# Splitting weights ahead of the norms, first activation parts ahead of weight splits, and context loads behind weight loads

## The reference

```
x   = x   + 0.5 * m[2]  * swiglu(modulate(rmsnorm(x,   norm_ffn1), m[0],  m[1]),  w_ffn1_in, w_ffn1_out)
ctx = ctx + 0.5 * mc[2] * swiglu(modulate(rmsnorm(ctx, norm_ffn1), mc[0], mc[1]), w_ffn1_in, w_ffn1_out)
px, pc = modulate(rmsnorm(x or ctx, norm_mix), ...) @ w_mix_in     # attention and short convolution
x   = x + m[5] * (mix @ w_mix_out)
x   = x + 0.5 * m[8] * swiglu(modulate(rmsnorm(x, norm_ffn2), m[6], m[7]), w_ffn2_in, w_ffn2_out)
x   = rmsnorm(x, final_norm)
# second block, with its own context ctx_2
feats = modulate(rmsnorm(x or ctx_2, norm1_w), ...) @ w_in          # retention and gated linear attention
x   = x + g1 * (y @ w_out)
x   = x + g2 * peer_ffn(modulate(rmsnorm(x, norm2_w), ...))         # 16 of 16,384 experts x 8 heads per token
out = rmsnorm(x, norm_f_w)
```

## Time and profile before

| What | us |
|---|---|
| median of three runs | 3168.67 |
| profiled execution, whole | 3173.42 |
| its span | 3171.6 |
| TensorE busy | 2752.9 (87%) |
| VectorE busy | 1723.3 (54%) |
| GpSimd busy | 1161.6 (37%) |
| ScalarE busy | 890.4 (28%) |

### The profile page before, as it was taken

The page is one execution under the profiler, slowest core; times in us unless marked ns, Lnnn a source line. Parts: engine busy times, 40 slices in busy tenths (PEclk is TensorE's granted clock), DMA queues, the critical chain, the costliest instruction groups (busy, mean ns, idle before and its releaser), DMA issues.

```text
span 3171.6 us, 30128 instructions
## 1 busy us (share of the span) xinstructions
PE 2752.9 (87%) x11118; PEld 1893.7 (60%) x11118; DVE 1723.3 (54%) x3643; ACT 890.4 (28%) x1683; POOL 1161.6 (37%) x763
## 2 busy tenths in 40 slices
PE   6899999989978999989987889988777777777876
PEld 4899989977657887778846665544333322222332
DVE  3777652032737603231146467766776777677765
ACT  3111123123533223242132333223322222222221
POOL 1222222223924444333210245445444444444442
PEclk8999999989998999989997899999999999999999
DMA  5455531212014523311100279999999999999997
GB/s 204 150 178 177 178 124 55 62 64 70 25 67 139 179 93 93 100 47 60 55 34 1 67 277 393 387 418 416 427 427 427 427 427 427 427 427 427 427 427 298
DMA packets 126957, 722.12 MB, mean 228 GB/s; under 512 B 15204, under 2 KB 17516, under 8 KB 60140
## 3 DMA queue, kind: packets, MB, share of 16 engines
q0 software_dynamic: 73728, 536.90, 40.6%
q1 hardware_dynamic: 37448, 127.67, 11.7%
q10 hardware_dynamic: 15652, 55.90, 5.6%
HBM read 718.31 MB, written 2.10 MB: 227 GB/s over the span
## 4 chain that ended last, share of the span: by engine, by line
PE 58%; DMA 26%; DVE 9%; ACT 3%; issue 3%; POOL 1%; SPq 0%; ACTq 0%; DVEq 0%; POOLq 0%
PE acc L582 14%; PE acc L583 13%; PE acc L584 13%; DMA wring<-in_peer_rows,squares 8%; DMA hid<-in_peer_rows,squares 8%; PE sums L1063 4%; DMA arena<-in_peer_rows,squares 4%; PE acc L1063 3%; DMA resid<-in_peer_rows,squares 3%; PE sums L515 2%; DMA modw<-in_peer_rows,squares 1%; DVE hid L1758 1%; ACT hid L1124 1%; DVE hid L2362 1%; DVE squares L1817 1%
## 5 line engine op out<-in xcount | busy, mean ns | idle before, releaser
L2527 POOL TENSOR_TENSOR wring_parts<-wring,wring_parts 128x1024 fp32r<-128x1024 f32 (+1 forms) x215 | 522.8, 2443 | 1269.6 <-ACT wring_parts L1124 1269.3
L582 PE MATMUL acc<-hid_parts,wring_parts 128*128 128x384 f32 (+2 forms) x2088 | 770.6, 369 | 56.1 <-DVE hid_parts L1764 31.4
L584 PE MATMUL acc<-hid_parts,wring_parts 128*128 128x384 f32 (+2 forms) x2088 | 753.4, 361 | 0.0
L583 PE MATMUL acc<-hid_parts,wring_parts 128*128 128x384 f32 (+1 forms) x1656 | 598.7, 362 | 0.0
L582 PEld LDWEIGHTS acc<-hid_parts,wring_parts 128*128 128x128 f32 (+1 forms) x2088 | 396.7, 190 | 118.4 <-issue 54.0
L584 PEld LDWEIGHTS acc<-hid_parts,wring_parts 128*128 128x128 f32 (+1 forms) x2088 | 396.3, 190 | 36.2
L1124 ACT ACTIVATE wring_parts<-wring 128x1024 fp32r<-128x1024 f32 (+1 forms) x215 | 222.2, 1040 | 567.4 <-DMA wring<-in_w_ffn_out 214.5
L583 PEld LDWEIGHTS acc<-hid_parts,wring_parts 128*128 128x128 f32 x1656 | 314.8, 190 | 33.2 <-issue 5.5
L2539 POOL DMA_INDIRECT arena<-in_peer_rows,squares x180 | 194.5, 1080 | 234.6 <-PE acc L1063 141.0
L1124 ACT ACTIVATE hid<-hid 128x2 f32<-128x2 f32 (+2 forms) x293 | 67.0, 229 | 759.7 <-DVE arena L2362 234.9
L2539 POOL DMA_INDIRECT wring<-in_peer_rows,squares x158 | 179.1, 1134 | 219.1 <-PE acc L1063 163.5
(11 more groups left out here) (408 smaller groups left out, 4440.4 us busy)
## 6 DMA issues: line engine op xcount, KB each, us to landing
wring<-in_w_ffn_in SPq DMA_DIRECT2D x88, 512.0 KB, 4.9
modw<-in_w_ada ACTq DMA_DIRECT2D x56, 512.0 KB, 3.9
modw<-in_w_mod ACTq DMA_DIRECT2D x48, 512.0 KB, 3.9
wring<-in_w_ffn_out SPq DMA_DIRECT2D x32, 512.0 KB, 3.5
wring<-in_w_in SPq DMA_DIRECT2D x28, 512.0 KB, 3.4
wring<-in_w_mix_in SPq DMA_DIRECT2D x18, 512.0 KB, 3.4
wring<-in_peer_w_q SPq DMA_DIRECT2D x16, 512.0 KB, 5.7
hid<-in_w_ada SPq DMA_DIRECT2D x6, 1024.0 KB, 16.8
```

The costliest lines, as they stand in the source:

```text
L582: nc.tensor.matmul(o, wh, high, start=first, stop=False)
L583: nc.tensor.matmul(o, wh, low, start=False, stop=False)
L584: return nc.tensor.matmul(o, wl, high, start=False, stop=last)
L2527: nc.gpsimd.tensor_tensor(Wlor[:, p, 0:blocks, 0:cols], Wlo[:, p, 0:blocks, 0:cols], Whir[:, p, 0:blocks, 0:cols], ALU.subtract).then_inc( ...
```

## The change

There are six edits.

1. **SyncE.** The load of the second context is passed to `ffn_in` as a function and called behind the first four tile loads of ffn2_in.
2. **Where high parts lie.** The two tiles of high parts in modw are now f = 2 and 3 instead of 18 and 19, and the early parts of the first stage are f = 0, 1, 2, 3. The hid tiles serve f = 4 to 19.
3. **Weight splits of ffn_out's chunks 2 and 3.** In both feed-forward stages they no longer follow the last silu; they stand behind the first four of the remaining parts in `ff_parts`.
4. **Weight splits at the norms.** The first two tiles of the next stage are split in `behind_chunks`, ahead of the squares of tiles 6 and 7. The other two: behind the shift of tiles 1 and 4 at the mix norm, and ahead of all squares at the second block's entry.
5. **Modulation quarters 0 and 1** are multiplied ahead of the wait for the first silu, instead of behind the first gating.
6. **The decay numbers** (18 small operations on 8 or 4 columns, VectorE L1892 to L1903) move from ahead of `swiglu` to behind the first stage's `ff_parts`.

```diff
         hi_ff768 = ([(tmp_parts[:, 0:HALF], tmp_parts[:, HALF:TC]), (rstd_parts[:, 0:HALF], rstd_parts[:, HALF:TC])]
+                    + [(modw_parts[:, TC * f:TC * f + HALF], modw_parts[:, TC * f + HALF:TC * (f + 1)]) for f in range(2)]
                     + [(hid_parts[:, TC * f:TC * f + HALF], hid_parts[:, TC * f + HALF:TC * (f + 1)]) for f in range(16)]
-                    + [(modw_parts[:, TC * f:TC * f + HALF], modw_parts[:, TC * f + HALF:TC * (f + 1)]) for f in range(2)]
...
-        EARLY_PARTS = {"ffn1_out": [0, 1, 18, 19], "ffn2_out": [0, 1, 2, 3, 4, 5]}
+        EARLY_PARTS = {"ffn1_out": [0, 1, 2, 3], "ffn2_out": [0, 1, 2, 3, 4, 5]}
...
-                    if j == 2 and weights is not None:
-                        high_part(weights)
+                    if j in weights:
+                        high_part(weights[j])
...
-                    if u % halves == halves - 1:
+                    if u % halves == halves - 1 and u < units * FT // 2 - 1:
                         for m in range(2):
                             high_part(s0 + W_RING + 2 * (u // halves) + m)
...
-                for f in PARTS[name][len(EARLY_PARTS[name]):]:
+                for i, f in enumerate(PARTS[name][len(EARLY_PARTS[name]):]):
+                    if i == 4:
+                        for q in range(2, W_RING):
+                            high_part(TILE_OF[name] + q)
...
-                for q in range(3 * j + W_RING, min(3 * j + W_RING + 3, OUT_TILES)):
+                for q in range(3 * j + W_RING, min(3 * j + W_RING + 3, OUT_TILES + 2)):
                     high_part(TILE_OF[name] + q)
...
-            stat(KD, TC, lambda j: behind_chunks("ffn1_out", j, TC), meanwhile=range(s0, s0 + W_RING), only=1)
-            shift(1, hi768r, lo768, 3 * KD, TC, 2)
+            stat(KD, TC, lambda j: behind_chunks("ffn1_out", j, TC), only=1)
+            shift(1, hi768r, lo768, 3 * KD, TC, 2, {1: s0 + 2, 4: s0 + 3})
...
-            stat(KD, TC, renormed, meanwhile=range(s0, s0 + W_RING))
+            for s in range(s0 + 2, s0 + W_RING):
+                high_part(s)
+            stat(KD, TC, renormed)
...
+                if first_pair == 0:
+                    mod_quarter(0)
+                    mod_quarter(1)
                 for u in range(2 * sides * FT // 2):
...
-                    if pair < stop_pair:
+                    if pair < stop_pair and (u or first_pair):
...
                 step(0)
+                behind_first()
                 with sp.Fori(1, FT // 2) as i:
                     step(i)
...
-            sp.wait_ge(acc_ready, UNIT["ffn2_in"])
-            for r in range(2):
-                sp.dma_start(tok2[:, r, :], a["ctx_2"][0][r * P:(r + 1) * P, :]).then_inc(tok2_loaded, 16)
-            ffn_in("ffn2_in", a["w_ffn2_in"], 1)
+
+            def second_context():
+                sp.wait_ge(acc_ready, UNIT["ffn2_in"])
+                for r in range(2):
+                    sp.dma_start(tok2[:, r, :], a["ctx_2"][0][r * P:(r + 1) * P, :]).then_inc(tok2_loaded, 16)
+            ffn_in("ffn2_in", a["w_ffn2_in"], 1, second_context)
```

More of the change, by code:

```diff
@@ L1173, in inverse, with shift @@
                 run(rstd[:, 0:t], logs[:, 0:t], ACT.Exp, scale=-0.5).then_inc(rstd_ready, 1)
-            def shift(norm, high, low, tile, t, stage, weights=None):
+            def shift(norm, high, low, tile, t, stage, weights={}):
                 act.wait_ge(mods_ready, stage)
@@ L1443, in _ @@
             behind("mix_out", x_, 0)
-            shift(2, hi512r, lo512, 6 * KD, T, 2, TILE_OF["ffn2_in"] + W_RING - 1)
+            shift(2, hi512r, lo512, 6 * KD, T, 2, {2: TILE_OF["ffn2_in"] + W_RING - 1})
             for x in range(2):
@@ L1599, in _ @@
             behind("w_out", x2_, 2)
-            shift(4, hi512r, lo512, ADA_TILES + 3 * KD, T, 3, TILE_OF["peer_q"] + W_RING - 1)
+            shift(4, hi512r, lo512, ADA_TILES + 3 * KD, T, 3, {2: TILE_OF["peer_q"] + W_RING - 1})
             def query(t):
@@ L1888, in _ @@
             scale(0, hi768r, lo768, lo768r, TC, 0)
+            swiglu("ffn1_in", HALF, 2, 0, 0, EARLY_PAIRS, "ffn1_out", ff768, hi_ff768, lo_ff768, 0)
+            ff_parts("ffn1_out", ff768, hi_ff768, lo_ff768, 0)
             dve.wait_ge(decay_exp, 1)
@@ L1903, in _ @@
             link(V.tensor_scalar(dec[:, 20:24], dec[:, 12:16], 640.0 + P, None, ALU.mult))
-            swiglu("ffn1_in", HALF, 2, 0, 0, EARLY_PAIRS, "ffn1_out", ff768, hi_ff768, lo_ff768, 0)
-            ff_parts("ffn1_out", ff768, hi_ff768, lo_ff768, 0)
             modulation(2, FIRST_GROUPS + EARLY_PAIRS, FIRST_MODS, EARLY_TILES, [(1, "norm_mix", 4 * KD), (2, "norm_ffn2", 7 * KD)],
@@ L2614, in stage_load, with ffn_in @@
                     tile_load(TILE_OF[stage] + t, w, t, P if t < w.shape[0] - 1 else last)
-            def ffn_in(name, w, halves):
+            def ffn_in(name, w, halves, behind_first=lambda: None):
                 s0 = TILE_OF[name]
```

## The result

The changed kernel takes 3137.27 us (median of 4 runs, 3128.56 to 3142.12); the kernel before, run beside it, 3170.18 (4 runs, 3161.62 to 3173.68). The ratio is 0.9896, 95% interval 0.9869 to 0.9923, so 1.0% faster. A second set on another occasion gave 3136.89 against 3171.69, ratio 0.9893 (0.9877 to 0.9911). The prediction was 3138.0 from a sum of 30.7 us. The profiled execution took 3140.62, 32.8 less than before's 3173.42, and it is read here.

A forecast was written before the change was run, and what follows sets the result against it. TensorE's holes were taken to bound the first 1,840 us, DMA transfers the rest. Terms 13.3 + 6.4 + 2.8 + 0.3 + 5.1 + 2.8 = 30.7 us, off the median 3168.7, gave 3138.0; range 3127 to 3153.

The forecast's parts named there:

- Edit 1, 13.3 taken: Behind mix_out: tile loads leave before the context load, so TensorE's sum starts sooner; gain 12.1 to 13.9 us, 13.3 taken.
- Edits 2 and 3 in ffn1_out, 6.4 taken: ffn1_out's first unit: more parts ready ahead of the hole, and no clock fall; gain 6.4 us, bounds 5.2 and 7.6.
- The hold-up near the end: ffn1_out: the split of chunk q = 4 blocks VectorE for one operation nearer the end; 0.6 us lost.
- Edit 3 in ffn2_out, 2.8 taken: ffn2_out: four parts now stand ahead of ScalarE's second split; gain 2.8 us, bounds 1.0 and 4.6.
- Edit 4a: Mix norm: first matmul 4.7 us earlier, but the third unit's hole grows to 5; net 0.3, bounds -1.4 and 1.2.
- Edit 4b: Second block's entry: earlier logarithm, scaling freed of two hold-ups; gain 5.1 us taken, bounds 1.0 and 5.5.
- The step that lets the sums start 0.8 later: Second block's entry: splits ahead of the squares meet VectorE's eight multiplications, adding 0.8 us to the start of the sums.
- Edits 5 and 6, 2.8 taken: Modulation quarters: their chain moves earlier and the later decay numbers cost nothing; gain 2.8 us, bounds 1.0 and 4.0.
- Rival (b): Whole kernel: shorter holes keep the clock at its upper level, every upper bound is reached; 3132 us, chance 0.08.
- Rival (a): Gains outside the context-load edit: GpSimd's weight splits block VectorE, shrinking them to about 3 us; 3152 us, chance 0.12.
- rival (c): Behind mix_out: the first tile's load still leaves only behind unit 7, losing 13.3 us; 3162 to 3168 us, chance 0.05.
- rival (d): Output stages and mix_out: ScalarE's waits for loads delay squares, slower from a landing of 46 us; 3180 us, chance 0.03.

The follow-up runs named there:

- edit 3 alone: The kernel before with only the feed-forward weight splits moved behind four parts, early parts still f = 0, 1, 18, 19; 3164.31 us, one run.
- 4b alone: The kernel before with only the second block's entry changed: two weight splits ahead of the norm, two ahead of its squares; 3174.09 us, one run.
- edits 2 and 3 alone: The kernel before with only the modw parts as f = 2 and 3 and the feed-forward weight splits behind four parts; 3161.44 us, one run.
- the two alone: The kernel before with only modulation quarters 0 and 1 ahead of the first silu and decay numbers behind the parts; 3175.08 us, one run.

## Why the prediction was right, step by step

**Edit 1, 13.3 taken, 15.1 measured (15.5 by leaving it out, 17.0 alone).** The mechanism was right: loads landed in 3.4 us, the near end of the landings taken. The size was off in two steps. I added up to a microsecond for the third split on GpSimd in the way of the last addition and for a late load; neither came, the hole is 2.23 and not 3.05 (16.35 - 13.3). And the clock: the sums took 2.07 us before and 1.13 now, another 0.9.

**Edits 2 and 3 in ffn1_out, 6.4 taken, 6.8 measured.** The hole fell by 7.01 - 1.84 = 5.2 and the clock stayed up, 1.6. The hold-up near the end that I took off (0.6) cannot be seen.

**Edit 3 in ffn2_out, 2.8 taken, 4.9 measured.** Four parts ahead of the splits shortened the hole by 2.6, the 2.8 of the step. The fall of the clock, which I had kept for the upper bound, went as well: 2.3. This term is mis-sized, and beyond its bound (4.6) by 0.3. That the fall went was luck: edit 3 alone kept it, behind the same hole.

**Edit 4a, 0.3 taken, 0.3 measured.** The hold-ups came where the step put them, at 2.1 us each (2.87 less 0.74), once on the way to the third unit's accumulators and once more; waits 4.35 and 4.67 where "4 to 5" and "about 5" were forecast. By the rule of the Trainium skill cited in the prediction (SBUF — State Buffer, "Who interferes with whom") the two kinds of instruction exclude each other. The trace agrees: each held operation ends about 0.5 us behind GpSimd's. The cost is the time for which they overlap, 2.1 us, since the operations started 0.1 to 0.4 us into GpSimd's 2.4 to 2.7. The full length would have given a loss of 0.3, and there was none.

**Edit 4b, 5.1 taken, 6.3 measured (5.6 by 4b alone).** The logarithm starts when the sums end (0.05 us behind, before 2.1), and the scaling has no operation over 1 us: the wait fell from 10.26 to 4.34. The step that lets the sums start 0.8 later, since the multiplications meet GpSimd, was right: they took 8.78 for 5.38, and the sums followed the first of them by 3.0 us instead of 1.7. In the profiled run this is hidden, as the multiplications themselves began 1.7 sooner behind the sum of ffn2_out, and the sums came 0.4 sooner, not later. That is the clock and not the edit. From the sum to the first multiplication, before, after, and in the second trace of the changed kernel:

```profile
1340.06:1346.12 6.06, 4.55 (x18) 3.17 (x18) 2.60 (x5) 1.32 (x2) 0.00 (x0) 0.72 0.33 132
```

```profile
1309.85:1314.22 4.37, 2.87 (x18) 2.10 (x18) 2.59 (x5) 3.18 (x4) 0.84 (x1) 1.00 0.44 178
```

```profile
1309.02:1314.94 5.92, 4.42 (x18) 3.04 (x18) 2.59 (x6) 3.21 (x4) 1.44 (x1) 0.73 0.33 134
```

TensorE waited 2.23 us ahead of this place in all three. With edits 2 and 3 alone, without 4b, the upper level lies here too, and the sums come 6.05 us behind ffn2_out's; after, they come 7.36 behind it. In the second trace of the changed kernel they come at 8.31, before at 7.73. So the hold-up costs 0.6 to 1.3 us, and I had taken 0.8. It follows that a part of the 6.3 is the clock's. With the lower level here f fell from 47.1 (before) to 41.4 (the second trace), by 5.7; with the upper one from 44.1 (edits 2 and 3 alone) to 40.8 (after), by 3.3. The 5.1 taken lies between the two.

**Edits 5 and 6, 2.8 taken, 3.4 measured (4.3 by the two alone).** Quarter 2 starts at 87.42, the load landing as worked out; the first sum stands at 115.80, forecast "near 116". The cover of the decay numbers held: b shows no trace of them.

**What the sum missed.** The terms came to 36.8 against the 30.7 taken, near 37, the sum of their upper bounds, though not term by term. Of these 6.1 us, 0.9 behind mix_out and 2.3 in ffn2_out are the clock, and a part of what 4b shows is too. Then 4.3 were given back between the entry and the expert queries, a stretch of which I had said nothing, because no edit touches it. The hit at 3137 to 3138 is in part these two cancelling, which is luck; that each hole fell for its own cause, and by about what was worked out, is not. Rival (b), the clock giving more, names much of what the terms had too little, but its 3132 did not come, since the clock also took back. Rival (a) is refuted by b, e and f, rival (c) by the hole of 2.23 (its bound was off besides: 3168.7 less 9 is 3160, not 3162), rival (d) by the landing of 3.4.

## What to carry to other kernels

An in-order queue is read by what stands behind its longest wait: the context load cost 15 us although nobody wanted it, as it stood ahead of tiles that everybody wanted. If a consumer starts early and then stands still, look whether the pieces that it gets first are those it asks for first; here the renumbering was worth more in ffn1_out (4.3 us) than the reordering (2.7). Judge an edit of a few microseconds by the stretch between two events around it, not by the whole time of one run: two edits here took 4 to 7 us out of their stretch, and their single runs were no faster than the kernel before.

## What was not expected of the hardware

- The same hole, about 2.1 us, was followed by the lower level of the clock in one kernel (0.59 over 4.2 us) and by the full one in another (1.00). Behind 1.90 us it fell (0.52 over 3.4 us), behind 2.07 (1350.68) it did not. Even two executions of one kernel differ: behind the wait of 2.23 us at the end of ffn2_out the granted clock up to the first multiplication was 1.00 in one trace of the changed kernel and 0.73 in the other. The hole of 1.90 us, before:

```profile
698.31 0.70 PE L582 MATMUL acc<-hid_parts,wring_parts 128*128 128x512 f32 x1 [1.90 <-ACT arena L1124]
```

- A stretch that no edit touches took 423.8 us twice in the kernel before, 428.1 and 427.7 in the changed one, and 433.5 in a kernel whose last edit stands some 900 us ahead of it. With an early edit the clock's lower level lies over other instructions much later; why is open.
